# A mixture-of-experts decoder block: the slot numbers of an expert's third row group dealt out another way

## The reference

```python
logits = (t @ w_router + b_router)                    # 512 tokens x 32 experts
top_logit, top_e = lax.top_k(logits, TOP_K)           # TOP_K = 4
gate = jax.nn.softmax(top_logit, axis=-1)
def expert_block(args):
    xb, e = args
    u = xb @ w_up[e] + b_up[e]                        # 1024 -> 2048
    glu = jnp.minimum(u[:, :D_FF], SWIGLU_LIMIT)
    lin = jnp.clip(u[:, D_FF:], -SWIGLU_LIMIT, SWIGLU_LIMIT)
    act = glu * jax.nn.sigmoid(SWIGLU_ALPHA * glu) * (lin + 1.0)
    return act @ w_down[e] + b_down[e]                # 1024 -> 1024
y = y_pad.reshape(cap, D)[dest] * gate[order][:, None]
return jax.ops.segment_sum(y, tok, num_segments=N)    # each token's four results are added
```

## Time and profile before

| | |
|---|---|
| median of 3 runs | 1533.33 us (1533.31 to 1534.19) |
| profiled execution, its time | 1533.36 us |
| its span, first to last instruction | 1531.6 us |
| TensorE busy | 1474.1 us (96%) |
| mean granted TensorE clock | 0.994 |
| bytes moved by DMA | 468.31 MB, 306 GB/s over the span |
| queue q1 (weights and other loads) | 443.71 MB, 70.2% of 16 engines' span |
| queue q0 (GpSimd's moves) | 22.93 MB, 5.6% |
| queue q8 (instruction fetches) | 87 packets, 0.4% |

### The profile page before, as it was taken

The page is one execution under the profiler, slowest core; times in us unless marked ns, Lnnn a source line. Parts: engine busy times, 40 slices in busy tenths (PEclk is TensorE's granted clock), DMA queues, the critical chain, the costliest instruction groups (busy, mean ns, idle before and its releaser), DMA issues.

```text
span 1531.6 us, 26598 instructions
## 1 busy us (share of the span) xinstructions
PE 1474.1 (96%) x10752; PEld 629.7 (41%) x10752; DVE 503.2 (33%) x1334; ACT 246.6 (16%) x554; POOL 172.4 (11%) x195
## 2 busy tenths in 40 slices
PE   9999999999999999998999999999999999999976
PEld 5444466544554434322334343343433334434322
DVE  3224345340214644322233222332323322233213
ACT  4013433411211111100011000101001100011002
POOL 1000000080001001110101111011110111101110
PEclk9999999999999999999999999999999999999999
DMA  6311042043062899999999999999999999999996
GB/s 252 106 59 55 1 144 77 1 156 112 11 264 90 337 358 402 414 421 412 408 419 411 414 420 408 412 416 416 421 411 415 418 419 421 415 416 420 419 414 246
DMA packets 59715, 468.31 MB, mean 306 GB/s; under 512 B 8922, under 2 KB 9022, under 8 KB 34800
## 3 DMA queue, kind: packets, MB, share of 16 engines
q1 hardware_dynamic: 48552, 443.71, 70.2%
q0 software_dynamic: 10976, 22.93, 5.6%
q10 hardware_dynamic: 72, 0.02, 0.0%
HBM read 454.33 MB, written 16.78 MB: 308 GB/s over the span
## 4 chain that ended last, share of the span: by engine, by line
PE 72%; DMA 23%; DVE 2%; issue 1%; ACT 0%; POOL 0%; SPq 0%; POOLq 0%; DVEq 0%; ACTq 0%
PE banks L866 25%; PE banks L933 17%; PE banks L988 9%; DMA ring<-in_w_up 7%; PE banks L955 7%; DMA ring<-in_w_down 5%; DMA arena<-h_rows,arena 4%; PE banks L998 3%; DMA x_res<-in_w_up 2%; DMA actT<-in_w_down 2%; DMA arena<-in_w_up 2%; PE banks L1169 1%; PE banks L1152 1%; PE banks L905 1%; PE banks L946 1%
## 5 line engine op out<-in xcount | busy, mean ns | idle before, releaser
L866 PE MATMUL banks<-ring,actT 128*128 128x512 f32 x448 | 198.6, 594 | 1.0 <-DVEq L471 1.0
L933 PE MATMUL banks<-arena 128*32 128x512 f32 x1712 | 190.0, 594 | 9.3 <-DMA arena<-in_w_up 9.3
L1913 DVE TENSOR_SCALAR tokA<-banks 64x512 f32<-64x512 f32 x64 | 43.7, 683 | 382.0 <-PE banks L933 375.1
L933 PE MATMUL banks<-ring,arena 128*32 128x512 f32 x1312 | 145.9, 593 | 1.9 <-DMA ring<-in_w_up 1.9
L752 POOL DMA_INDIRECT arena<-h_rows,arena x31 | 32.9, 1062 | 803.9 <-DVE arena L1884 767.8
L866 PEld LDWEIGHTS banks<-ring,actT 128*128 128x128 f32 x448 | 83.0, 191 | 93.8 <-issue 91.4
L933 PEld LDWEIGHTS banks<-arena 128*32 128x32 f32 x1712 | 53.1, 110 | 128.5 <-issue 113.1
L988 PE MATMUL banks<-ring,arena 128*32 128x512 f32 x768 | 97.8, 620 | 3.3 <-DMA ring<-in_w_down 3.3
L1478 ACT ACTIVATE tokA<-tokA 128x512 f32<-128x512 f32 x32 | 20.2, 630 | 478.8 <-DVE tokA L1913 478.8
L988 PE MATMUL banks<-arena 128*32 128x512 f32 x704 | 89.2, 606 | 0.5 <-DMA arena<-in_w_down 0.5
L866 PE MATMUL banks<-actT,ring 128*128 128x512 f32 x192 | 83.5, 593 | 0.0
(11 more groups left out here) (399 smaller groups left out, 1709.9 us busy)
## 6 DMA issues: line engine op xcount, KB each, us to landing
arena<-in_w_up SPq DMA_DIRECT2D x50, 2048.0 KB
ring<-in_w_up SPq DMA_DIRECT2D x48, 2048.0 KB
ring<-in_w_down SPq DMA_DIRECT2D x24, 2048.0 KB
arena<-in_w_down SPq DMA_DIRECT2D x22, 2048.0 KB
x_res<-in_w_up SPq DMA_DIRECT2D x15, 2048.0 KB
actT<-in_w_up SPq DMA_DIRECT2D x15, 2048.0 KB
x_res<-in_w_down SPq DMA_DIRECT2D x9, 2048.0 KB
actT<-in_w_down SPq DMA_DIRECT2D x8, 2048.0 KB
```

What stands on the lines that cost most here:

```text
L866: mm = pe.matmul(o, lhsT, rhs, start=(k == 0), stop=(k == KT - 1))
L933: mm = pe.matmul(bank[g][32 * t:32 * t + 32, :], lhsT, w[:, 512 * t:512 * t + 512], start=False, stop=(k == KT - 1))
L1913: v.tensor_scalar(gluA[64 * g:64 * g + 64, :], bank[g][0:64, :], LIMIT, None, ALU.min).then_inc(gluA_ready, 1)
```

## The change

One line: the pattern of the eight `iota` instructions that number B's slots. Their count, shapes and order stay, and on every engine the program's instructions stand in the same order as before. The set of ranks is the same too; only their places differ.

```diff
                 for q in range(4, 8):
                     for u in range(2):
                         every2nd = t[:, :, 32 * q:32 * q + 32].rearrange("p j (h a u) -> p j h a u", a=8, u=2)[:, :, :, :, u]
-                        g.iota(every2nd, pattern=[[W, blocks], [1 - 2 * u, 2], [-2 + 4 * u, 8]], base=WIDE + 14 + 3 * u,
+                        g.iota(every2nd, pattern=[[W, blocks], [-16, 2], [2 * u - 1, 8]], base=WIDE + 16 + 7 + u,
                                channel_multiplier=0, allow_small_or_imprecise_dtypes=True).then_inc(iota_ready, 1)
```

## The result

Seven runs of the changed kernel have a median of 1540.12 us (1538.42 to 1542.39), seven of the kernel before on the same chip 1534.72 (1533.31 to 1535.46). The ratio is 1.0036, 95% interval 1.0027 to 1.0046: 5.5 us slower (4.1 to 7.0). Two later measurements of the same kernel gave 1.0036 (1.0023 to 1.0049) and 1.0042 (1.0027 to 1.0057). The forecast of 1537.4 had the sign and most of the mechanism; the time lies 2.7 us above it and 0.5 us above its range. Half of the 2.7 is not the change: the kernel before has 1534.7 us in this measurement, where the sum started from 1533.4. The other half is the effect: 5.4 us between the medians (5.5 by the ratio) instead of 4.0.

What follows compares the result with a forecast made beforehand. The prediction took the end to be bound by DMA, by the slowest late engine's row packets. Base 1533.4 us plus 4.0 us for engine 9, nothing for the rest, gave 1537.4 us; own range 1536.4 to 1538.8, full range 1534.2 to 1539.6.

Steps and rivals of the forecast that it cites:

- What bounds the kernel, and that a late engine's own sum counts: Expert part's end: bound by DMA, waiting for the slowest engine, whose own sum of packet times moves the last landing.
- The rival that TensorE hides it: Last 100 us bound by TensorE's own work, so later weights vanish in part: 1533 to 1535.5 us; 8%.
- Slots 2e and 2e + 1 on one engine: B's gathers and scatters: neighbouring slots 2e and 2e + 1 belong to engine e, in both half rows.
- a dealing to which I gave 3%: Rival dealing of B's packets: four slots such as 28 to 31, with both half rows, on one engine; 3%.
- A dealt by rank modulo 8, each over two engines: A's rows: dealt by rank modulo 8 over engines e and e + 8, not changed by the edit.
- The late half is 7 and 9 to 15: End of the weights: instruction fetches go round engines 7 and 9 to 15, about 7 us each, making them late.
- The rival with the late half the other way round: Late engines are 0 to 6 and 8, or 0 to 7; the slowest loses 14 rows, 3.3 us: 1530.1 us; 6%.
- The step that failed: what engine 9's rows cost: Engine 9 gets 20 rows of B more, 4.7 us, and ends 4.0 us later than engine 10 did; bounds 3.2 to 4.3.
- the recorded prices: Cost of a filled B slot on its engine: 0.08 us in the gather, 0.153 in the scatter, together 0.233.
- The gathers' waits, taken as 0 with 1 us for the upper end: TensorE's 8 waits for gathers: up to 1.3 us more, taken as 0 while the weights queue is full.
- The base: Starting level for the sum, the time of the kernel before: 1533.4 us.
- What would show it: Signs: DMA share 1.01, then about 0.5 for some 4 us longer either side; TensorE busy unchanged, waits 4 us more.

Runs made afterwards that it cites:

- heavy_9: Kernel before, but engine 9 alone has 38 rows of B, engines 3 and 4 lighter in exchange: 1538.55 us, ratio 1.0030, 4.6 us slower.
- heavy_10: Kernel before, but ranks 0 and 1 together on engine 10, engines 7 and 15 lighter in exchange: 1539.98 us, ratio 1.0042, 6.4 us slower.
- run 14: Not a follow-up: one expert's pass inside the kernel, with 16 B rows.
- run 21: Not a follow-up: one expert's pass inside the kernel, with 8 B rows.
- run 11: Not a follow-up: one expert's pass inside the kernel, with 21 B rows.
- quick8: Against the kernel before, ranks 0 to 15 on engines 0 to 4, 7, 8 and 15: 1530.53 us, ratio 0.9974, 4.0 us faster.
- run 31: Not a follow-up: one expert's pass inside the kernel, with 37 tokens.
- low_on_quick: Against the kernel before, ranks 0 to 15 on engines 0 to 5, 8 and 15: 1534.65 us, ratio 1.0005, 0.8 us slower.
- graded: Against the kernel before, ranks 18 to 31 on engines 6 and 9 to 14, different loads on the other nine: 1530.83 us, ratio 0.9980.
- heavy_10b: Kernel before with ranks 0 and 1 on engine 10, measured once more: 1539.58 us, ratio 1.0040, 6.1 us slower.
- heavy_3: Kernel before, but ranks 0 and 1 together on engine 3, engines 7 and 15 lighter in exchange: 1533.35 us, ratio 0.9999, no change.
- run 30: Not a follow-up: the expert's pass at the end of the kernel's chain; its down weights landed at 1502.12 us before, 1508.69 after the change.

## Why the prediction was right in kind and low in size

- **What bounds the kernel, and that a late engine's own sum counts**: right. Same packets, other engine: 6.4 us on engine 10, nothing on engine 3. The rival that TensorE hides it is out: 4.6 us for heavy_9, 6.4 for heavy_10, and the change itself costs 5.5.
- **Slots 2e and 2e + 1 on one engine**: right. The sizes of B's packets in the trace of before show it: 32 with one row (2052 bytes) in run 14; 16 with one row and 16 empty ones (8 bytes) in run 21; 10 full and 22 with one row in run 11. So do the strings: those that can be followed without a gap have two packets of B behind four of A, and run 14's 32 and 64 packets are that for all 16; in run 11 five strings have two full ones, in run 21 eight have two empty ones. The lone engine that each probe moved fits it too, and quick8's table, laid out by it, had its landing 4.1 us sooner where 4.3 was expected. With the four slots 28 to 31 and both their half rows on one engine, a dealing to which I gave 3%, that engine would go from 44 rows to 70 with the change, 26 x 0.233 = 6.1 us: 1539.5 us, nearer to the measured time than the forecast is. It is out all the same: it would leave B's packets to eight engines, where the strings of all 16 have them, and the lags of the sixteen engines in eight profiles are off by over 3 us under it and by 0.76 under this one. That its time came close is chance.
- **A dealt by rank modulo 8, each over two engines**: the trace bears it out. Run 31's 37 tokens make 32 full, 10 single-row and 22 empty packets. Six strings have two full and two empty ones; the other ten share the rest, in the nine that can be followed without a gap two full, one with one row, one empty. That is what this dealing gives for 37 ranks. That the two are e and e + 8 rests on the fit.
- **The late half is 7 and 9 to 15**: six of eight. It is 5, 6 and 9 to 14. Engines 7 and 15, which have the fewest rows of A, are quick ones by the fit. It made no difference to this forecast, since 9 and 10 belong to both sets and decide. In the design of a better table one engine taken wrongly costs nearly as much as the change: low_on_quick, which spares engine 7 where quick8 spares 5, is 4.8 us behind quick8. Engine 15 does not decide either: graded, with 48 rows on it, is 3.1 us faster.
- **The rival with the late half the other way round**: out; its sign is wrong.
- **The step that failed: what engine 9's rows cost.** The sum had 20 x 0.233 - 0.7 = 4.0 us, with nothing for the weights packets beside the rows; the measured effect is 5.5 us (4.1 to 7.0), and 5.1 to 6.6 in landings. The price of a row on an engine that is heavy alone was near enough: (4.6 + 0.7) / 20 = 0.27 in heavy_9 (the 0.7 is what engine 9 had less than engine 10 before), and 6.4 and 6.1 us for 26 gather and 30 scatter rows in heavy_10 and heavy_10b, 0.22 to 0.23 each, where the recorded prices give 6.7; the lags of all engines give 0.26 to 0.29. That puts the step at 3.7 to 5.1 us, and heavy_9 alone measured 4.6. The rest is a term that the sum put at nothing without a reason: the weights packets of the change took 20 us more over 16 engines, 1.3 us each by the estimate above. That this is what makes up the difference fits in size; it is not shown by a run.
- **The gathers' waits, taken as 0 with 1 us for the upper end**: right at 0. They are 17.2 us in 8 waits against 16.9 in 8, and heavy_3, with four filled slots on one engine in most runs, costs nothing.
- **The base, 1.3 of the 2.7 us.** The sum started from the profiled execution and the median of three runs, 1533.4. The kernel before had medians of 1534.7, 1533.7, 1533.6, 1534.4 and 1533.8 us in the five measurements here. A range of ±1 us for the level of before alone was missing; with it 1540.1 would have lain inside.
- **What would show it**: run 14's packets, the bytes and the waits came as said (waits for weights 4.3 us more, 4 expected). TensorE's busy time, said to be unchanged, is 3.6 us longer in this execution. The picture at the end did not: no two levels but steps to 1516 us, since the change makes the eight late engines unlike (34 rows or more for 9 to 14, 6 to 8 for 5 and 6).

## What to carry to other kernels

In this kernel, with a DMA share of 1.01 from 600 us on the earlier trace rows, the down weights of run 30 landed with the last of the 16 engines: 7.3 us later when ranks 0 and 1 were put on engine 10 alone. The mean share over 100 us hides that. Look at how the share falls at the end (0.36 in the change's profile is about six engines of 16 still at work, 0.07 in heavy_10's about one), and at who does side work there. Try to give the engines with the least other work what is dealt by slot: here the same rows of B, 344 gathered and 350 scattered, were worth 5.5 us lost or 4.0 us won by their slots alone. To learn which engine is which, put one lump on one engine at a time, or loads of different sizes on all engines in doubt; here the table of before, with 18 to 26 rows of B on every engine, showed a late half but not who is in it. Look at what happens to the packets beside the ones that you move, and not only at these. And give the base its own share of the range.

## What the hardware showed that was not expected

- The eight late engines are 5, 6 and 9 to 14 by their B slots (the fit, off by 0.76 us), not one half of the sixteen. By the transfers around 1440 us they are 10.9 us behind the others (by the fit); the fetches and the long weights packets behind them give an estimate of 11.3 us by 1490. That these eight carry the fetches, and that the fetches are the cause, is read from the packets and not tried.
- Two filled slots on one engine are one packet of 4 KB in a gather (0.160 us; 4096 bytes in the trace) and two of 2 KB in a scatter (0.173 us each).
- Leaving out B's gather rows everywhere (22 on engine 10) makes run 30's down weights land 5.0 us sooner, 0.23 us a row, though 26 gather rows more on one engine cost it 0.06 each. Without these rows the weights packets are shorter by 64 us over 16 engines, 0.19 us for each of the 344 rows, where the rows' own packets take 0.09. Why they hold up the weights is not shown.
- The end of a transfer of 2 MB comes from one engine alone for up to 8 us (heavy_10), at 25 GB/s from 1512 to 1514 us, where the sixteen together move 416.
